# Prompt attention of a decoder step: the mask added by DVE in the maximum pass, search rounds spread between maxima, and another order of the query tiles

## What is computed

```python
dots = einsum('bqhd,bsd->bqhs', qi, ki)                      # indexer, 8 heads
s = einsum('bqhs,bqh->bqs', relu(dots), wi * IDX_SCALE)      # one score per query and key
s = where(k_pos <= q_pos, s, -inf)
_, idx = top_k(s, 256)                                       # 256 keys per query
s = einsum('bqngd,bqknd->bqngk', qg, k_sel) * 64 ** -0.5
p = softmax(where(valid, s, -inf)); o = einsum('bqngk,bqknd->bqngd', p, v_sel)
```

## Time and profile before

| | |
|---|---|
| median of the runs | 6136.24 us |
| the profiled execution | 6147.33 us |
| its span, first to last instruction | 6145.7 us |
| busy in the span | PE 76%, DVE 37%, ACT 30%, POOL 11% |
| prompt attention in it | 679 to 2879 us, 2200 us |
| busy in that stretch | PE 1709, DVE 1150, ACT 1046, POOL 221 us |

### The profile page before, as it was taken

How to read it: one execution, slowest core, us unless ns; L and a number is a source line. 1 busy time by engine, 2 the same in 40 slices (tenths; PEclk the granted TensorE clock), 3 DMA queues, 4 the chain that set the end, 5 groups by cost and what they waited for, 6 DMA issues and landing times. The chain is left out here.

```text
span 6145.7 us, 54949 instructions
## 1 busy us (share of the span) xinstructions
PE 4685.9 (76%) x15814; PEld 2443.1 (40%) x15868; DVE 2258.1 (37%) x5087; ACT 1825.2 (30%) x3166; POOL 659.1 (11%) x798
## 2 busy tenths in 40 slices
PE   7999545667788998887744999828788785589980
PEld 2444112222333333333334444316556554444430
DVE  1111374444555545662524001054434442411105
ACT  0111124556565655222111122212222321112212
POOL 0111210000001000011021000120000000100013
PEclk9999667788999999999865999959898885589995
DMA  6111100000000000000535777560010001347865
GB/s 250 53 52 43 56 21 12 12 6 12 7 13 13 13 13 13 13 11 24 195 121 215 278 279 265 214 251 21 20 41 21 20 21 41 128 171 270 290 240 192
DMA packets 153248, 603.55 MB, mean 98 GB/s; under 512 B 24576, under 2 KB 27008, under 8 KB 134121
## 3 DMA queue, kind: packets, MB, share of 16 engines
q1 hardware_dynamic: 97946, 407.29, 18.7%
q0 software_dynamic: 34208, 119.30, 5.5%
q10 hardware_dynamic: 20928, 75.00, 3.0%
HBM read 466.97 MB, written 134.61 MB: 98 GB/s over the span
## 5 line engine op out<-in xcount | busy, mean ns | idle before, releaser
L2190 PE MATMUL experts_ps_gu<-w_sb,experts_xT 128*128 x1504 | 677.5, 604 | 45.9 <-DMA w_sb<-moe_w_in 41.4
L996 PE MATMUL attend_po<-attend_PT,V 128*128 128x512 f32 x1088 | 572.3, 652 | 9.0 <-ACT attend_total L741 9.0
L768 ACT ACTIVATE attend_passed<-attend_score,attend_cand 128x1024 bf16<-128x1024 f32 (+8 forms) x279 | 439.3, 1575 | 356.9 <-DVE attend_cand L868 333.2
L2707 PE MATMUL recurrent_psAB<-recurrent_hT,rec_w_in_sb 128*128 128x256 f32 (+1 forms) x2304 | 536.1, 392 | 10.6 <-ACT recurrent_hT L2502 10.6
L468 PE MATMUL project_pj<-project_w,project_hT 128*128 128x512 f32 (+2 forms) x1360 | 507.8, 531 | 6.6 <-ACT project_proj L384 5.5
L2707 PEld LDWEIGHTS recurrent_psAB<-recurrent_hT,rec_w_in_sb 128*128 128x128 f32 x2304 | 463.6, 215 | 77.0 <-issue 11.8
L811 DVE TENSOR_REDUCE attend_mx<-attend_aux 128x1 f32<-128x512 f32 (+3 forms) x640 | 365.0, 606 | 278.5 <-PE attend_aux L1007 271.5
L2190 PEld LDWEIGHTS experts_ps_gu<-w_sb,experts_xT 128*128 128x128 f32 x1504 | 284.3, 194 | 374.1 <-issue 374.1
L1006 PE MATMUL attend_aux<-attend_hide,attend_identb 128*128 128x512 bf16 (+3 forms) x587 | 223.7, 384 | 244.2 <-DVE attend_mx L811 231.5
L731 ACT ACTIVATE attend_PT<-attend_big 128x512 f32<-128x512 f32 x544 | 292.5, 589 | 366.1 <-PE attend_big L985 365.4
L2180 PE MATMUL experts_ps_y<-w_sb,experts_midT 128*128 x752 | 343.0, 599 | 11.4 <-issue 11.4
(11 more groups left out here) (465 smaller groups left out, 5793.4 us busy)
## 6 DMA issues: line engine op xcount, KB each, us to landing
w_sb<-moe_w_in SPq DMA_DIRECT2D x64, 2048.0 KB, 11.7
w_sb<-moe_w_in SPq DMA_DIRECT2D x64, 1024.0 KB, 8.5
yb_scratch<-experts_y ACTq DMA_DIRECT2D x94, 512.0 KB, 8.3
index_slab<-ada_w_in SPq DMA_DIRECT2D x12, 2048.0 KB, 9.7
route_x<-xa_scratch SPq DMA_DIRECT2D x32, 512.0 KB, 4.6
hs_scratch<-route_h ACTq DMA_DIRECT2D x32, 512.0 KB, 4.8
yb_scratch<-route_blank SPq DMA_DIRECT2D x32, 512.0 KB
combine_x<-xa_scratch SPq DMA_DIRECT2D x32, 512.0 KB, 4.6
```

The costliest lines, as they stand in the source:

```text
L768: act.activation(passed[:, 0:L[m]], score[:, m % 2, 0:L[m]], ACT.Sign, bias=threshold, accum_out=balance[:, :]).then_inc(balanced, 1)
L996: pe.matmul(po[:, n % 2, :], V1[:, b, n, :], PT[:, g % 4, :], start=(b == 0), stop=(b == S[i] // NKV - 1)).then_inc(pv_done, 1)
L2190: last = pe.matmul(ps_gu[:, u, :], xT[:, u, k, :], w1[:, bass.ds(slot, 1), k, :].rearrange("p a n -> p (a n)"), start=(k == 0), stop=(k == ...
L2707: last = pe.matmul(psAB[:, c % 2, part, 0:W], w_in[:, k, part * D + c * P:part * D + (c + 1) * P], hT[:, k, 0:W], start=(k == 0), stop=(k ...
```

## The change

DVE adds the mask as it takes the maximum: `tensor_tensor_reduce` reads the score from `aux` and the mask from `hide`, adds them, writes the sum to `junk`, and leaves the largest. PE's product of the mask with the identity goes. The zero rows in `qTb` go too; a unit's product has 64 rows, and two heads that lie in different halves of the rows are filled as a pair (`unit_pair`), one into each bank. PE no longer waits for the mask.

DVE's work of a slot is dealt into parts, one for each pair of maxima and each pair of indexer sums (`parts_at`), and the slot's search rounds are dealt over the parts (`rounds_at`), ahead of each part's sums or maxima. ACT's counts are dealt out in the same way among its `rectify` pairs. Pieces from 33 on stand at the end of the slot. ACT's copies of the tile before move behind slot 0's counts, but where a step has a single slot.

`TILE` becomes 1, 4, 8, 12, 15, 14, 13, 11, 10, 9, 7, 6, 5, 3, 2, 0. `narrow` becomes one copy of 128 partitions.

```diff
-        qTb = sb("qTb", [P, H, P], BF16)
+        qTb = sb("qTb", [P, H // 2, P], BF16)
+        junk = sb("junk", [P, 2, 512], BF16)
-        TILE = [0] + list(range(1, NT, 2)) + list(range(NT - 2, 0, -2))
+        RAMP = [1, 4, 8, 12]
+        TILE = RAMP + [t for t in range(NT - 1, -1, -1) if t not in RAMP]
-        def units_at(i, s):
-            return share_of(U[i + 1], s, 0, max(middle(i), 1)) if there(i + 1) else range(0)
+        def unit_pairs_at(i, s):
+            return share_of(U[i + 1] // 2, s, 0, max(middle(i), 1)) if there(i + 1) else range(0)
+        def unit_pair(m, v):
+            jg, c = divmod(v, CUTS[m])
+            return jg // GQ, jg % GQ, c, slice(512 * c, min(512 * c + 512, L[m]))
+        def parts_at(i, s):
+            return max(len(unit_pairs_at(i, s)) + len(pairs_at(i, s)), 1)
+        def rounds_at(i, s, n, of):
+            rounds = pieces_at(i, s)
+            rounds = range(rounds.start, max(min(rounds.stop, 33), rounds.start))
+            return rounds[len(rounds) * n // of:len(rounds) * (n + 1) // of]
...
-                pool.memset(qTb[:, :, :], 0.0).then_inc(consts, 1)
...
-                    for r in range(2):
-                        pool.drain()
-                        pool.tensor_copy(qTb[r * DH:(r + 1) * DH, :, :].rearrange("p (j r g) q -> p r j (g q)", r=2, g=GQ)[:, r],
-                                         qT[r * DH:(r + 1) * DH, m % 3].rearrange("p (j g) q -> p j (g q)", g=GQ)).then_inc(qTb_ready, 1)
+                    pool.tensor_copy(qTb[:, :, :], qT[:, m % 3]).then_inc(qTb_ready, 1)
...
-                        if s == 0 and there(i - 1):
+                        if s == 0 and there(i - 1) and middle(i) == 0:
                             copy_out(i - 1, 1)
...
-                        for pair in pairs_at(i, s):
-                            rectify(i + 3, pair)
-                        if there(i + 2) and by_act(i + 2):
-                            for r in pieces_at(i, s):
-                                if r < 31:
-                                    weigh(i + 2, r)
+                        for n in range(parts):
+                            if units <= n < units + len(pairs):
+                                rectify(i + 3, pairs[n - units])
+                            if there(i + 2) and by_act(i + 2):
+                                for r in rounds_at(i, s, n, parts):
+                                    if r < 31:
+                                        weigh(i + 2, r)
+                        if s == 0 and there(i - 1) and middle(i) > 0:
+                            copy_out(i - 1, 1)
...
-                    h, c = divmod(u, CUTS[m])
-                    wide = min(512, L[m] - 512 * c)
+                    j, g, c, keys = unit_pair(m, u // 2)
+                    h = (2 * j + u % 2) * GQ + g
+                    wide = keys.stop - keys.start
+                    if u == 0:
+                        dve.wait_ge(hidden, m + 1)
                     dve.wait_ge(unit_filled, sum(U[:m]) + u + 1)
-                    dve.tensor_reduce(mx[:, h, c:c + 1], aux[:, u % 2, 0:wide], AX.X, ALU.max).then_inc(maxed, 1)
+                    dve.wait_ge(maxed, sum(U[:m]) + u + 1)
+                    dve.tensor_tensor_reduce(junk[:, u % 2, 0:wide], aux[:, u % 2, 0:wide], hide[:, keys], 1.0, LOWEST,
+                                             ALU.add, ALU.max, mx[:, h, c:c + 1]).then_inc(maxed, 1)
...
-                                dve.wait_ge(unit_filled, sum(U[:m]))
...
-                        for u in units_at(i, s):
-                            largest(i + 1, u)
-                        if there(i - 1):
-                            for part in normal_at(i, s):
-                                normalise(i - 1, part)
-                        if s == middle(i) and there(i + 3):
-                            scale_weights(i + 3)
-                        for pair in pairs_at(i, s):
-                            add_up(i + 3, pair)
-                        if there(i + 2):
-                            for r in pieces_at(i, s):
+                        for n in range(parts):
+                            for r in rounds_at(i, s, n, parts):
+                                search(i + 2, r)
+                            if n < len(units):
+                                largest(i + 1, 2 * units[n])
+                                largest(i + 1, 2 * units[n] + 1)
+                            if n == 0 and there(i - 1):
+                                for part in normal_at(i, s):
+                                    normalise(i - 1, part)
+                            if n == min(len(units), parts - 1) and s == middle(i) and there(i + 3):
+                                scale_weights(i + 3)
+                            if len(units) <= n < len(units) + len(pairs):
+                                add_up(i + 3, pairs[n - len(units)])
+                        for r in pieces_at(i, s):
+                            if r > 32:
                                 search(i + 2, r)
...
-                    pe.wait_ge(maxed, sum(U[:m]) + u + 1)
-                    pe.matmul(aux[:, u % 2, 0:n], identb4[:, 0, :], hide[:, keys], start=True, stop=False)
-                    pe.matmul(aux[:, u % 2, 0:n], qTb[:, h, :], KTb[:, h // GQ // 2, keys], start=False, stop=True).then_inc(unit_filled, 1)
+                    for half in range(2):
+                        r = rows_of_half(half)
+                        pe.wait_ge(maxed, sum(U[:m]) + 2 * v + half + 1)
+                        pe.matmul(aux[:, half, 0:keys.stop - keys.start], qTb[r, j * GQ + g, :], KTb[r, j, keys],
+                                  start=True, stop=True).then_inc(unit_filled, 1)
```

30 lines of the change are left out of this document (16 added, 14 removed).

## The result

The changed kernel takes **5932.67 us** (median; 5920.19 to 5937.58), the kernel before 6138.19 us on the same chip: ratio 0.9665 [0.9653, 0.9677], 205 us faster. The forecast was 84 us faster. The time lies inside the range of 5930 to 6140, at the value of rival D (5934), and not near the 6054 of case A. The profiled execution took 5920.19 us.

The account below looks back on a forecast made before the run. A search ring of DVE, ACT and PE was taken to bound the attention: new bounds of 1827 us plus excess gave a 2123 us stage, less 5 elsewhere, 82 under 2200, so 6054 us; range 5930 to 6140.

Parts of the forecast that it names:

- rival D: Prompt attention: the engines' coupling goes wholly, taking 120 us of the 296 us excess, giving 5934 us; chance 0.20.
- case A: Prompt attention: ACT's chain sets first halves and the excess shrinks, giving 6054 us, within 5990 to 6110; chance 0.50.
- the kept excess: Attention half steps: time over the largest engine sum, such as 140 us in the ramp and 128 on the way down.
- the forecast's end part: Steps after the downward ones: bounds of 46.8, 37.5, 24.9 and 16.7 us, excess -3, together 123 us.
- their bounds: Attention half steps: the largest engine's summed work at full clock; over all steps of the change 1827 us.
- 7 us over the chain: First halves bound by ACT's search rounds: 7 us excess each, against 7.4 to 34.7 in steps 2 to 10 before.
- The 13 us charged for it: Searches of tiles 6, 5, 3, 2 in steps 9 to 12: 112 dearer maxima on DVE's path add 13 us.
- DVE's 8.3 us: DVE's work in a step: normalising costs 8.3 us, four operations of 1.74 and a product.
- The ring of three engines: Attention search: waits of 333.2, 250.1 and 271.5 us among ACT, DVE and PE are one ring, not three losses.
- B: DVE-bound steps 9 to 12: a lighter PE runs at a lower clock, +76 us, giving 6130; chance 0.15.
- B's sign: Last DVE-bound steps, 9 to 12: a granted clock over 0.85 was expected, else the cold-PE rival holds.
- C: Rounds over ACT: a pair of maxima between two rounds delays each of 279, +140 us at 0.5, giving 6194; chance 0.15.

Follow-up runs that it names:

- no_t: The changed kernel with the old order of tiles: 5916.15 us, ratio 0.9648 to the kernel before.
- r_only: The kernel before with rounds dealt, normalising moved, outputs copied later and fills counted by pairs; mask on PE, old tile order: 5937.25 us, ratio 0.9674.
- dve_slow: no_t with a drain and two idle 128x128 additions on DVE behind every pair of maxima: 6022.66 us, ratio 0.9799 to the kernel before.

## Why the prediction was wrong

**What failed: the kept excess.** The forecast set the time of a half step as the largest engine sum plus an excess carried over from before, shrunk by judgement. With the end of before's stage put right (36 us more, which the forecast's end part then has too), forecast and measurement by part are:

| part | forecast | measured |
|---|---|---|
| start, up to step 0 | 120 | 104.5 |
| ramp, steps 0 to 3 | 632 | 598.4 |
| down, steps 4 to 12 | 1248 | 1149.8 |
| end | 123 + 36 | 169.5 |

The sum is 137 us too high. The first halves carry most of it. In the down part their bounds sum to 623, I added 51, and they took 602; in the ramp 292 plus 28 against 298. So the "7 us over the chain" had no cause of its own, and once the turn-taking is gone nothing of it is seen in the sums. Second halves: ramp 312 forecast and 301 measured, down 573 and 548. There the excess was about right in the ramp and a third too large in the way down; that dealing also serves the second halves (53 to 68 us in the old order) was priced in no step of the prediction.

**What was mis-sized: the maximum.** 0.75 was 0.61 to 0.62 with its read. The lower end was right. The 13 us charged for it in the steps bound by DVE are part of the 21 us by which the first halves of the down part fell below their bounds; the other 8 I can't place. The pair of fills was taken at 0.21 us and stands at 0.32 to the next pass.

**What was missed: the order of fills, and the normalising.** Together they are worth 62 us. The working priced the fills as lighter and did not ask where they stand: counted by pairs, fewer of them stand ahead of PE's product in the slots with six maxima, and the product no longer waits behind one that DVE's rounds hold up (by the estimate above about half of the 62). It listed the normalising among DVE's 8.3 us and did not ask what stands behind it: in before a reciprocal of 1.74 stands between the last maximum and the round for which ACT waits. The diff moves it in front of all but one pair of the slot.

**What was right.** The ring of three engines was named as the cause, and the chip agrees: its waits carry the gain. The light fill of PE was valued at nothing on the path and the mask's change is worth 21 us beside the rest. DVE's wait for PE at a maximum was foretold under 100 and just missed it (102.1). Nothing of the order of tiles stood in the likeliest sum as a gain (38 us of bounds more), and it is worth nothing. But the wait for ACT's count was foretold under 150 and is 295: I had the side wrong on which the slack would show. DVE now has time over, which is what a chain over ACT at its bound means.

**The rivals.** B (no gain by a cold PE): the clock of the way down is 0.96 as before, but the prediction had set B's sign at a clock of 0.85 in the steps bound by DVE. Their first halves (steps 9 to 12) were granted 0.91, 0.90, 0.81 and 0.79, so the sign appeared in two of four. The first and the last of them, and the second half of step 12:

```profile
2091.00:2163.00 72.00, 52.12 (x156) 16.89 (x154) 64.75 (x170) 14.85 (x31) 3.10 (x3) 0.91 0.03 10
2442.00:2491.00 49.00, 33.99 (x93) 11.06 (x92) 42.40 (x140) 10.49 (x22) 2.25 (x3) 0.79 0.04 13
2491.00:2529.00 38.00, 34.24 (x127) 15.80 (x125) 13.11 (x38) 14.23 (x34) 9.50 (x6) 1.00 0.08 29
```

PE was 69 to 72% busy in these two first halves, not the 34 to 41% that B had worked out. The rule that the prediction took from the Trainium skill (TensorE: Matmul & The Clock Gate, "Part 1: The HAM clock gate") agrees with the sag, with the ramp, where PE is 67% busy and was granted 0.74, and with the first halves of no_t beside r_only (0.86 for 0.91). But B's price did not come: the first halves are bound by DVE (65 of 72 us busy), and the second halves of steps 9 to 12, which B put at 282 us, were granted 1.00 and took 185. C (slower): not here; dve_slow comes out at C's size, 59 of its 96 us at most in C's way. D (the coupling goes wholly) is the case that came. It had the time right within 2 us by luck, since its parts were wrong: it left second halves 85 us of excess and they have 152; it left first halves 26 and they have 15 less than nothing. It deserved the larger chance, since the prediction itself had named the ring as the only cause of the excess and then kept half of it.

## What to carry to other kernels

Where three engines hand work round in order, sum what each half of the loop would take with no hand-over at all, and take that as the forecast unless a wait of its own can be named for what is added to it. Follow each queue past what a change moves: a fill that must wait held up a product behind it, and a reciprocal that nobody waits for stood ahead of a round that ACT waited for; together they were 62 of 205 us. And check what else the kernel of a single part carries: 96 and 62 us gave 100 together, and both kernels had the new order of fills in them, so neither was the price of its part alone.

## What the runs showed of the hardware

- An addition and a maximum in one custom pass on DVE, one operand in PSUM in f32 and one in SBUF in bf16, with a bf16 result written, costs no more than the plain maximum over the same 512 (mean 687 ns in before): mean 689 ns, 0.61 us from start to start in a row, the 83 ns read of the accumulator inside it.
- Two bf16 passes of 512 columns on 64 rows each, on different halves of the rows, do run at the same time. In the changed kernel a pair lasts 0.38 to 0.39 us from its first start to its last end, as one such pass alone does, and a pass of 128 rows starts 0.31 to 0.32 us after the pair and after the single pass alike. First a pair, then a pass by itself:

```profile
1397.12 0.39 PE L1034 MATMUL attend_aux<-attend_KTb,attend_qTb 64*128 64x512 bf16 x2
1397.44 0.61 PE L1007 MATMUL attend_big<-attend_half_bias,attend_half_hide 128*128 128x256 bf16 x4
...
1408.99 0.39 PE L1034 MATMUL attend_aux<-attend_KTb,attend_qTb 64*128 64x512 bf16 x1 [0.23 <-DVE attend_mx L834]
1409.31 1.12 PE L1025 MATMUL attend_po<-attend_PT,V 128*128 128x512 f32 x2
```

  Of 216 pairs whose passes stand by themselves in the rows, 113 start within 20 ns of each other; in 75 the second starts over 0.4 us later, as at 1408.99, where it waits for DVE to free its bank. The forecast took 0.21 for the pair.
- The product with values of one slot took 3.62 us in before (1254.43) after PE had stood for 6.95 us with a short fill between, against 1.98 in the earlier trace rows. Slow ones remain with the rounds dealt: no_t has one of 3.55 us at 1205.68 in the same step. The granted clock of that half step was 0.75 in before and 0.84 in no_t.
